# Two transformer blocks on one NeuronCore: where the splits of late weight chunks stand around the gate and up stage

## What is computed

```
h = h + jnp.concatenate([o_g, o_f], axis=-1) @ w_out[i]      # output projection ("wo2")
hn = rmsnorm_2(h, ffn_norm_w[i])
gate, up = jnp.split(hn @ w_gate_up[i], 2, axis=-1)          # D_FF = 2816
h = h + (jax.nn.silu(gate) * up) @ w_down[i]                 # down projection ("dn")
```

## Time and profile before

| | |
|---|---|
| median of 3 runs | 1196.85 us (1196.37 to 1197.42) |
| the profiled execution | 1197.8 us, span 1196.0 us |
| PE busy | 1169.2 us, 98% of the span |
| DVE busy | 756.1 us, 63% |
| ACT busy | 554.5 us, 46% |

### The profile page before, as it was taken

One profiled execution on the slowest core, in us unless ns is written; L12 is line 12 of the kernel. 1 busy time (PEld: TensorE's weight loads), 2 busy tenths in 40 slices (PEclk: granted clock), 3 DMA queues, 4 the chain that ended last, 5 costly groups with the idle time before them and its releaser, 6 DMA issues.

```text
span 1196.0 us, 17906 instructions
## 1 busy us (share of the span) xinstructions
PE 1169.2 (98%) x7362; PEld 986.6 (82%) x7362; DVE 756.1 (63%) x1197; ACT 554.5 (46%) x886; POOL 94.4 (8%) x114
## 2 busy tenths in 40 slices
PE   7999999999999999999999999989999999999997
PEld 5888778787777887887777788879999999888886
DVE  6776455566557765648886884487767676444455
ACT  6416524536544455115447535465555555322254
POOL 0190021111000100100000200000000000100000
PEclk9999999999999999999999999999999999999999
DMA  9862189999612434981222001135656565633321
GB/s 373 306 222 91 53 306 299 241 295 301 164 53 72 143 99 156 315 217 53 58 80 75 19 4 36 51 109 199 224 178 194 176 194 172 238 97 97 101 84 75
DMA packets 57792, 185.97 MB, mean 155 GB/s; under 512 B 6544, under 2 KB 6672, under 8 KB 52592
## 3 DMA queue, kind: packets, MB, share of 16 engines
q1 hardware_dynamic: 47088, 127.29, 32.0%
q0 software_dynamic: 9776, 56.10, 17.2%
q10 hardware_dynamic: 848, 1.45, 0.3%
HBM read 178.52 MB, written 52.43 MB: 193 GB/s over the span
## 4 chain that ended last, share of the span: by engine, by line
PE 86%; DVE 5%; ACT 4%; DMA 2%; issue 1%; ACTq 0%; DVEq 0%
PE pb L752 83%; DMA raw<-w_all 2%; PE pb L1015 1%; PE pb L843 1%; DVE wlo L2060 1%; ACT whi L1501 1%; ACT Y L1501 1%; DVE xT L2060 1%; DVE xqs L2063 0%; DVE xlo L2060 0%; PE pb L1176 0%; DVE tmpf L2060 0%; ACT xhi L1501 0%; DVE ssq L2060 0%; ACT xq L1501 0%
## 5 line engine op out<-in xcount | busy, mean ns | idle before, releaser
L2060 DVE TENSOR_TENSOR wlo<-raw,whi 128x1024 fp32r<-128x1024 f32 (+1 forms) x210 | 256.7, 1224 | 120.7 <-ACT whi L1501 119.9
L752 PE MATMUL pb<-hhi,wlo 128*128 128x512 f32 (+2 forms) x696 | 270.3, 388 | 2.6 <-DVE wlo L2060 2.6
L752 PE MATMUL pb<-hhi,whi 128*128 128x512 f32 (+2 forms) x696 | 269.7, 388 | 0.0
L752 PE MATMUL pb<-hlo,whi 128*128 128x512 f32 (+2 forms) x696 | 268.3, 394 | 0.7 <-DVE tmpf L2060 0.7
L1501 ACT ACTIVATE whi<-raw 128x1024 fp32r<-128x1024 f32 (+1 forms) x210 | 214.6, 1037 | 83.9 <-DMA raw<-w_all 64.7
L752 PE MATMUL pb<-xlo,whi 128*128 128x256 f32 x616 | 175.8, 285 | 4.9 <-issue 1.9
L752 PE MATMUL pb<-xhi,whi 128*128 128x256 f32 x616 | 175.0, 284 | 0.0
L752 PE MATMUL pb<-xhi,wlo 128*128 128x256 f32 x616 | 175.0, 284 | 0.0
L752 PEld LDWEIGHTS pb<-hhi,wlo 128*128 128x128 f32 (+1 forms) x696 | 130.4, 187 | 30.5 <-DVE wlo L2060 3.5
L752 PEld LDWEIGHTS pb<-hlo,whi 128*128 128x128 f32 (+1 forms) x696 | 130.3, 187 | 30.3 <-issue 3.3
L752 PEld LDWEIGHTS pb<-hhi,whi 128*128 128x128 f32 (+1 forms) x696 | 130.3, 187 | 27.4
(11 more groups left out here) (417 smaller groups left out, 1869.8 us busy)
## 6 DMA issues: line engine op xcount, KB each, us to landing
raw<-w_all SPq DMA_DIRECT2D x121, 512.0 KB, 4.4
w_sums<-w_all POOLq DMA_DIRECT2D x30, 1024.0 KB, 14.2
raw<-w_sums SPq DMA_DIRECT2D x88, 256.0 KB, 2.9
raw<-w_all SPq DMA_DIRECT2D x66, 256.0 KB, 3.1
w_sums<-w_sums POOLq DMA_DIRECT2D x10, 1024.0 KB, 11.3
adab<-ada_d SPq DMA_DIRECT2D x12, 512.0 KB, 11.9
gbt<-ada_d SPq DMA_DIRECT2D x12, 512.0 KB, 7.3
raw<-w_all SPq DMA_DIRECT2D x13, 384.0 KB, 3.1
```

Of the source, the lines that this page charges most:

```text
L752: return e.matmul(out, lhs, rhs, start=start, stop=stop, skip_group_check=True)
L2060: return e.tensor_tensor(out, a, b, op)
```

## The change

On ACT and DVE the call `conv("wo2", 3)` in front of the residuals is taken out. On ACT the call behind `fifth(1)` asks for one chunk more. On DVE the last pass of the loop over units leaves out its split and its read of (2, 21), and these come behind the loop in another order.

```
@@ scalar_program
             for m in range(4):
                 A.wait_ge(*VD(("go", 3)))
                 copy(hhi3[:, m, :], gzs[:, m, :]).then_inc(HI.sem, 1)
-            conv("wo2", 3)
...
             fifth(1)
-            conv_for(6, 0)
+            conv_for(7, 0)
             root(rsb[:, :], 7, D, "ffn")
@@ vector_program
                 low(("3", m), hlo3[:, m, :], gzs[:, m, :], hhi3[:, m, :])
-            conv("wo2", 3)
...
                 gated_up(u - 1)
-                conv_for(2, u)
-                gate_early(u)
                 if u < FFB - 1:
+                    conv_for(2, u)
+                    gate_early(u)
                     act_low(u - 1)
+            gate_early(FFB - 1)
             up_late(FFB - 1)
+            conv_for(2, FFB - 1)
+            gate_late(FFB - 1)
             act_low(FFB - 2)
-            gate_late(FFB - 1)
             conv("st", len(PRODUCTS) // 2 - 1)
```

## The result

The changed kernel takes 1191.27 us (median of 5, 1190.34 to 1191.48) against 1196.46 us for the kernel before in the same measurement (median of 5, 1196.37 to 1197.42). The ratio is 0.9951, with a 95% interval of 0.9940 to 0.9962: 0.4 to 0.6% faster. The forecast was 1190.75 with a range of 1189.4 to 1193.0. The profiled execution has a span of 1189.5 us, against 1196.0 (forecast 1189.9).

A forecast was written before the change was run, and what follows sets the result against it. PE, busy for 98% of 1196.0 us, was taken as the bound, losing only to waits and a lowered clock. 3.0 + 1.5 - 0.2 + 0.9 + 0.9 = 6.1 us off the median 1196.85 gave 1190.75, range 1189.4 to 1193.0.

The forecast's parts named there:

- The chain of residuals: Residual stage on ACT and DVE: with two splits moved, the last residual starts 3.0 us earlier.
- The clock: PE near 800 us, behind two waits around (6, 0): granted clock no longer falls to 1.2 GHz, winning 1.5 us.
- `third_seed(0)`: DVE's operation that PE needs for (7, 0): late next, costing 0.2 us that the low clock used to hide.
- Rival 1: PE near 800 us: the clock falls all the same, gain 4.8 us, 1192.05; chance 0.20.
- The wait ahead of (4, 0): PE's wait for the low half of its weights, 809.76 to 810.69: claimed gone, 0.9 us.
- Rival 2: Residual stage: the two moved splits cost the chain all they freed, total gain 2.4 us, 1194.45; chance 0.08.
- Rival 3: SP's queue: the load of st 0 comes too late and holds up ACT and the chain, 1200.6 us; chance 0.03.
- Rival 4: DVE: the residual of block 0 starts no earlier because something else holds DVE, gain 1.8 us, 1195.05; chance 0.03.
- The end: End of gate and up on DVE: up_late(21) runs ahead of the split of dn 0, winning 0.9 us.
- D: PE's wait for up_late(21) ahead of (4, 21), 1016.70 to 1017.59: claimed gone, 0.9 us.
- The likeliest case: Whole kernel: the summed gain of 6.1 us, 1190.75 us, own range 1189.6 to 1191.8; chance 0.62.
- C: PE's wait ahead of (4, 0) for the low half of its weights: claimed gone, 0.9 us.

The follow-up runs named there:

- e4: Kernel before with only the split of wo2 5 moved behind the residuals on both engines, wo2 4 left ahead: 1193.70 us, ratio 0.9977.
- e5: Changed kernel with the call for the splits of wo2 4 and 5 put back on ACT alone: 1194.24 us, ratio 0.9979.
- e1: Kernel before with only the new order of the last reads and the split of dn 0 on DVE: 1196.37 us, ratio 0.9997.
- e2: Kernel before with only ACT's split of st 5 moved ahead of the root: 1195.04 us, ratio 0.9988.
- e11: Kernel before with the new order of the last reads, and SP's load of dn 4 held until the parked activations land: 1196.07 us, ratio 0.9993.
- e12: Control: kernel before with only SP's load of dn 4 held until the parked activations land: 1196.84 us, ratio 0.9997.
- e8: Changed kernel with DVE's split right behind the residual in blocks 0 to 3, and the plr loads held back: 1190.60 us, ratio 0.9946.
- e3: Kernel before with only the call for the splits of wo2 4 and 5 ahead of the residuals removed on both engines: 1192.57 us, ratio 0.9968.
- e9: Changed kernel with SP's load of dn 4 held until the parked activations have landed: 1190.30 us, ratio 0.9941.
- e7: Changed kernel with the four plr loads on POOL held back until the first block of the down projection is done: 1189.58 us, ratio 0.9945.
- e6: Changed kernel with DVE's split in blocks 0 to 3 moved to where DVE waits for ACT's scaling: 1190.11 us, ratio 0.9946.

## Why the prediction was right, and where not

**The chain of residuals: right.** Predicted 3.0 us earlier, measured 3.24 (35.14 against 31.90 behind T0). The steps were 3.85 and 4.34, predicted 3.9 and 4.4. That it began with the first residual, and not with the products, is shown by e4 and e5: what starts the first step or two late comes out at the last one, to a tenth (1.60 in e4, 2.72 in e5). e5 also shows that ACT's queue counted as much as DVE's: with ACT's call back in place only 0.5 is left.

**The clock: right in kind, a little too large.** The 1.5 less the 0.2 of `third_seed(0)` made 1.3 net. T0 to the sum of squares went from 45.10 to 40.70, so 4.40 - 3.24 = 1.16, or 1.44 with the 0.28 of `third_seed(0)`. The four other traces with both old waits, e1, e2, e11 and e12, show the low clock too and lose 0.9 to 1.2 by it (their sums of squares come 44.85 to 45.12 behind T0; without the low clock it would be 45.10 - 1.16 = 43.94). The nine traces with less idle time show 1.00 throughout. Rival 1 did not happen. The rule that I had set beside it, on brief and frequent waits, from the Trainium skill, "TensorE: Matmul & The Clock Gate", section "A second HAM failure mode: psum-queue depth-cycling", found no agreement here: the waits that were left near 800 us did not bring the clock down in any of these nine.

**`third_seed(0)`: right.** Predicted 0.2, measured 0.28.

**The wait ahead of (4, 0): right.** Predicted 0.9, measured 1.02 in e2 with the restart.

**The other rivals.** Rival 2 had 0.6 for the chain, it gained 3.24. Rival 3 had the load of `st` 0 hold it up, but the steps of blocks 4 to 6 still take 4.98 to 4.99 us. Rival 4 had the first residual no earlier, it starts with T0.

**The end: this step failed.** I wrote "D is gone: 0.9". It is gone, and worth 0.99 up to the first matmul of the down projection. But I checked only the split of `dn` 0 and `act_low(20)` as what might be late next, not the transfers that the moved split lets go. The load of `dn` 3 waits for the low half of `dn` 0. It used to leave 2.7 us ahead of the first `aR` transfer (issued at 1019.58) and now leaves 1.6 ahead (of 1012.52), and the one of `dn` 4 slips from the same moment to half a microsecond behind. SP's timeline, before:

```profile
1016.89 0.33 SPq L609 DMA_DIRECT2D raw<-w_all  x1
...
1019.62 0.33 SPq L609 DMA_DIRECT2D raw<-w_all  x1
```

and after:

```profile
1010.96 0.33 SPq L609 DMA_DIRECT2D raw<-w_all  x1
...
1013.03 0.33 SPq L609 DMA_DIRECT2D raw<-w_all  x1
```

By stretches, the transfer engines of the changed kernel run full there (1.08 is their share, 402 the GB/s):

```profile
1016.00:1024.00 8.00, 8.00 (x37) 1.00 1.08 402
```

They are as full in the kernel before (1.08 and 409 GB/s from 1023 to 1031 us), so the load as a whole doesn't tell the two orders apart.

The ten traces without the hold fall into two groups: the six with the last part of the change (after, e1, e5 to e8) have longest landings of 10.7 to 11.7 us, the four without it (before, e2, e3, e4) 9.6 to 9.9. PE waits in every trace of the first group and in none of the second. Net of the wait the end gave 0.99 - 0.63 = 0.36 in the changed kernel and less than nothing in e1. Shown is that the weight loads from `dn` 4 on cause the late landing (e9 to e12: 7.1 at most) and that those of `plr` do not (e7). That it is the shift of `dn` 3 and not another effect of the new order that lifts 9.7 to 11 is argued from the issue times only, and no run moved that load by itself. e11 and e12 narrow it: with the loads from `dn` 4 on held back, `dn` 3 leaves 1.56 ahead of the first `aR` transfer in one and 2.69 in the other, and both have 7.1. So the shift of `dn` 3 lengthens the longest landing at most together with the later loads; the half microsecond by which `dn` 4 itself slipped is as likely a cause. This stays open.

**The sum.** T0 to the down projection 6.40, predicted 6.1; with the wait on `aR` 5.77; medians 5.2 apart, and by the ratio 5.9 (0.0049 x 1196), 4.5 to 7.2 at the ends of its interval. These agree. The likeliest case held. That the sum came within 0.3 us of the trace is partly luck: the end fell short by 0.54 (0.36 instead of 0.9), and the chain and C made up 0.24 and 0.12 of it.

## What to carry to other kernels

An in-order engine that is only 63% busy can still be the bound: the splits cost nothing in busy time, but each waited for a later product, and work that was ready stood behind them on both engines. Place such a wait behind the last piece of work that is ready without it, and fill with it the gap in which the engine waits for its partner anyway (e6). And when a split or a read moves, follow the transfer that it lets go, not only the engines: here weight loads that PE was not waiting for delayed transfers with half a microsecond to spare (a landing of 9.9 us cost nothing, one of 10.7 did).

## What the hardware showed beyond that

The granted clock fell behind waits of 1.9 and 1.5 us with 1.1 us of matmuls between them, in all five traces that have them. It did not fall behind 1.4 and 1.5 us in the same place in the one trace that has these (e5), nor behind 0.3 and 1.5 (e4). Half a microsecond less of standing still in e5 thus went with some 1.2 us less of low clock behind it: its sum of squares comes 1.68 earlier than before, and the chain gives 0.52 of that.

Every execution has another history ahead of T0. In the changed kernel's trace the stretch from 30 to 60 us ran at 0.90 of the full clock, in that of before at 1.00. The stretch from 700 to 755 us went the other way, 1.00 in the changed kernel's trace and 0.97 in that of before. No one stretch explains T0, which lies earlier in the changed kernel's trace, for all its slower start. T0 moved by 4 us between executions, while the same stage measured from T0 came out equal to 0.03 us (253.21 to 253.24 in after, e7 and e9). Counting from a common event in the trace told edits of half a microsecond apart that five rounds of medians could not.
